# A two-block transformer in float32 on one core: the low part of h's tile 0 gets the same home and the same order of products as the other tiles

## What is computed

```
h = rmsnorm(x, g) * (1 + scale) + shift          # scale, shift, gate from a small product with c
FFN:    y = (silu(h @ w_gate) * (h @ w_up)) @ w_down          # inner width 2816
mixers: y = mixer(h @ w_in) @ w_out
x = x + gate * y
```

## Time and profile before

| | us |
|---|---|
| median of 3 runs | 1773.77 |
| lowest and highest | 1773.6, 1774.51 |
| the profiled execution | 1783.76 |
| its span, first to last instruction | 1782.0 |

### The profile page before, as it was taken

The page is one execution under the profiler, slowest core; times in us unless marked ns, Lnnn a source line. Parts: engine busy times, 40 slices in busy tenths (PEclk is TensorE's granted clock), DMA queues, the critical chain, the costliest instruction groups (busy, mean ns, idle before and its releaser), DMA issues.

```text
span 1782.0 us, 34261 instructions
## 1 busy us (share of the span) xinstructions
PE 1742.4 (98%) x14686; PEld 1699.3 (95%) x14686; DVE 1452.5 (82%) x1750; ACT 956.5 (54%) x1254; POOL 0.2 (0%) x4
## 2 busy tenths in 40 slices
PE   5999999999999999999999999999999999999999
PEld 4999999998999999999999999999999998989999
DVE  7799899988898879897558989765899888567776
ACT  4444566676533454445765333566655556675553
POOL 0000000000000000000000000000000000000000
PEclk9999999999999999999999999999999999999999
DMA  9999734443798859895436988343387545316550
GB/s 395 411 420 332 308 143 166 166 144 141 313 394 328 331 204 389 326 379 183 149 141 227 387 309 352 147 154 124 127 302 282 210 147 187 141 72 218 186 199 34
DMA packets 68149, 426.23 MB, mean 239 GB/s; under 512 B 7488, under 2 KB 10832, under 8 KB 31824
## 3 DMA queue, kind: packets, MB, share of 16 engines
q1 hardware_dynamic: 63936, 416.22, 61.3%
q10 hardware_dynamic: 4112, 8.62, 1.4%
HBM read 423.74 MB, written 3.17 MB: 240 GB/s over the span
## 4 chain that ended last, share of the span: by engine, by line
PE 93%; DVE 3%; ACT 3%; DMA 1%; issue 0%; DVEq 0%; SPq 0%; ACTq 0%
PE bank L1575 25%; PE bank L1576 24%; PE bank L1577 24%; PE bank L1632 2%; PE bank L1634 2%; PE bank L1633 2%; PE bank L1588 1%; PE bank L1688 1%; PE bank L1602 1%; PE bank L1991 1%; DMA mix<-mods 1%; PE bank L1591 1%; ACT w_hi L496 1%; PE bank L1859 1%; ACT work L719 0%; PE bank L1972 0%
## 5 line engine op out<-in xcount | busy, mean ns | idle before, releaser
L1575 PE MATMUL bank<-h_hi,w_hi 128*128 128x256 f32 x2504 | 696.2, 278 | 0.0
L1577 PE MATMUL bank<-h_hi,w_lo 128*128 128x256 f32 x2504 | 695.2, 278 | 0.0
L1576 PE MATMUL bank<-h_lo_rest,w_hi 128*128 128x256 f32 x2504 | 695.2, 278 | 0.0
L915 DVE TENSOR_TENSOR w_lo<-raw,w_hi 128x2048 fp32r<-128x2048 f32 x267 | 609.5, 2284 | 91.4 <-ACT w_hi L496 90.4
L496 ACT ACTIVATE w_hi<-raw 128x2048 fp32r<-128x2048 f32 x276 | 527.9, 1913 | 159.7 <-PE bank L1577 146.1
L1575 PEld LDWEIGHTS bank<-h_hi,w_hi 128*128 128x128 f32 x2504 | 473.0, 189 | 0.0
L1576 PEld LDWEIGHTS bank<-h_lo_rest,w_hi 128*128 128x128 f32 x2504 | 470.2, 188 | 0.0
L1577 PEld LDWEIGHTS bank<-h_hi,w_lo 128*128 128x128 f32 x2504 | 470.1, 188 | 0.0
L1575 PE MATMUL bank<-a_hi,w_hi 128*128 128x256 f32 x1280 | 358.6, 280 | 0.8 <-DVE a_lo L1293 0.8
L1577 PE MATMUL bank<-a_hi,w_lo 128*128 128x256 f32 x1280 | 355.4, 278 | 0.0
L1576 PE MATMUL bank<-a_lo,w_hi 128*128 128x256 f32 x1280 | 355.4, 278 | 0.0
(11 more groups left out here) (304 smaller groups left out, 1986.3 us busy)
## 6 DMA issues: line engine op xcount, KB each, us to landing
raw<-weights SPq DMA_DIRECT2D x276, 1024.0 KB, 5.3
modws<-mods SPq DMA_DIRECT2D x144, 768.0 KB, 6.7
mix<-mods SPq DMA_DIRECT2D x5, 1024.0 KB, 8.8
mix<-mods ACTq DMA_DIRECT2D x8, 512.0 KB, 13.3
biases<-scratch ACTq DMA_DIRECT2D x1, 2048.0 KB, 13.3
mix<-biases ACTq DMA_DIRECT2D x4, 512.0 KB, 3.8
modws<-mods SPq DMA_DIRECT2D x1, 1024.0 KB, 11.6
x<-xin SPq DMA_DIRECT2D x1, 1024.0 KB, 10.9
```

What stands on the lines that cost most here:

```text
L915: eng.tensor_tensor(w_lo[g % NW][:, :], raw[g % NRAW][:, :], w_hi[g % NW][:, :], ALU.subtract).then_inc(sems["wlo"], 1)
L1575: eng.matmul(dst, ah, bh, start=start, stop=False, skip_group_check=skip)
L1576: eng.matmul(dst, ah, bl, start=False, stop=False, skip_group_check=skip)
L1577: return eng.matmul(dst, al, bh, start=False, stop=stop, skip_group_check=skip)
```

## The change

The low parts of all eight tiles lie in one array `h_lo_all`, tile 0 first, so that tile 0 starts at a step of 1024 bytes like the others and tiles 1 to 7 start 1024 bytes later than before. The two gaps become one of 64 floats, and everything behind keeps its address. `gemm` calls `three` for tile 0 too, in both forms. All other lines are the same.

```diff
-        h_lo_rest = sb("h_lo_rest", [P, KT - 1, T], F32R)
-        gap = sb("gap", [P, 16])
-        h_lo_first = sb("h_lo_first", [P, T], F32R)
-        gap2 = sb("gap2", [P, 48])
+        h_lo_all = sb("h_lo_all", [P, KT, T], F32R)
+        gap2 = sb("gap2", [P, 64])

         def h_lo(kk):

-            return h_lo_rest[:, kk - 1, :] if kk else h_lo_first[:, :]
+            return h_lo_all[:, kk, :]
...
-        z_hi, z_lo = h_hi[:, 1:3, :], h_lo_rest[:, 0:2, :]
+        z_hi, z_lo = h_hi[:, 1:3, :], h_lo_all[:, 1:3, :]
...
-                            if tokens and kk == 0:
-                                eng.matmul(d, h_lo(kk)[:, part], hi[:, kk, :], start=True, stop=False)
-                                eng.matmul(d, h_hi[:, kk, part], hi[:, kk, :], start=False, stop=False)
-                                eng.matmul(d, h_hi[:, kk, part], lo[:, kk, :], start=False, stop=False)
-                            elif tokens:
+                            if tokens:
                                 mm = three(d, h_hi[:, kk, part], h_lo(kk)[:, part], hi[:, kk, :], lo[:, kk, :],
                                            kk == 0, kk == KT - 1)
-                            elif kk == 0:
-                                eng.matmul(d, hi[:, kk, part], h_lo(kk), start=True, stop=False)
-                                eng.matmul(d, hi[:, kk, part], h_hi[:, kk, :], start=False, stop=False)
-                                eng.matmul(d, lo[:, kk, part], h_hi[:, kk, :], start=False, stop=False)
                             else:
                                 mm = three(d, hi[:, kk, part], lo[:, kk, part], h_hi[:, kk, :], h_lo(kk),
                                            kk == 0, kk == KT - 1)
```

## The result

| | before | with the change |
|---|---|---|
| median | 1773.97 us (7 runs) | 1792.91 us (7 runs) |
| lowest and highest | 1773.49, 1779.46 | 1780.36, 1794.63 |
| profiled execution, its span | 1783.76, 1782.0 | 1792.91, 1791.1 |
| ratio, 95% interval | | 1.0082 [1.0063, 1.0100] |

The changed kernel is slower, by 0.8% or 14.5 us by the ratio. (The runs of the changed kernel spread over 14 us: four lie between 1792.9 and 1794.7, three between 1780.3 and 1788.7. The ratio is smaller than that of the two medians, 1.0107.) The spread itself is new: six of the seven runs of the kernel before lie between 1773.49 and 1774.7.

A forecast was written before the change was run, and what follows sets the result against it. TensorE, busy 98% of the span, was taken as the bound, through the pace of its matmul starts. Terms -1.1 -1.9 +10.6 -6.4 +4.0 gave +5.2 us on 1773.8: 1779.0 us, range 1764 to 1792.

The forecast's parts named there:

- The mechanism: FFN stages run wholly at a fast or slow pace, 5.3 us apart; tile 0's 64-byte shift switches it.
- the home could not matter: Inference from TensorE's two independent read ports: the change does nothing, 1773.8 us; chance one in fifteen.
- (b): Tile 0's triplet in fast FFN stages: 0.027 us saved each time, 1.1 us for stage 9.
- rival 3: Slower by more: stages 2 and 5 slow, stage 9 slow, or mixers lose re-starts: 1785 to 1792; 0.52 together with forecast.
- (c): Mixers: 94 half-products, some 70 in fast pace, save 0.027 us each: 1.9 us saved.
- (d): Stages 3 and 7 enter slow, nothing turns them fast at L1602, no stall: +5.3 us each, +10.6.
- (e): Stages 2 and 5 enter fast, stall about 0.1 us, then pace open; one of two taken as fast: -6.4 us.
- (f): Stage 0 stays slow to its end without the triplet, if it gets slow at that point again: +4.0 us.
- The sum against the profiled execution: All terms added against the profiled execution's own time of 1783.76 us: +5.2 us.
- I move the difference over unchanged: Profiled execution is 10 us above the runs' median; its +5.2 is applied to 1773.8, giving 1779.0.

The follow-up runs named there:

- e1: Kernel before with tile 0's home kept 64 bytes off, its triplet in plain order (h_hi, h_lo, h_hi): 1776.59 us, ratio 1.0013.
- e2: Changed kernel (low parts in line) with tile 0's triplet issued low part first, as before the change: 1798.85 us, ratio 1.0134.
- e5: Kernel before without the gap: tile 0 keeps its own array and order but lies at a whole 1024-byte step: 1785.21 us, ratio 1.0069.
- e6: Kernel before with the gap doubled, so tile 0 lies 128 bytes off a step instead of 64: 1808.19 us, ratio 1.0193.
- e4: Changed kernel, unedited, profiled a second time: 1799.03 us in one run, five slow stages.
- e8: Changed kernel plus one 64-byte-shifted matmul ahead of each of the first two plain half-products, every stage but the first: 1790.96 us, ratio 1.0084.
- e7: Changed kernel plus one 64-byte-shifted matmul ahead of the first plain half-product of every stage but the first: 1789.35 us, ratio 1.0079.
- e9: Changed kernel plus two matmuls ahead of the low parts of each opening product but stage 0's, to fill TensorE's wait: 1797.53 us, ratio 1.0113.
- e3: Kernel before, unedited, profiled a second time: 1773.36 us in one run, no slow stage.
- e10: Kernel before with plain order in products going to bank 4 (gates), low part first in all others: 1775.24 us, ratio 0.9995.

## Why the prediction was right, and where its sum was not

The sign and the cause were right: slower, by paces that the shifted tile no longer ends. By the ratio the time is 1788.5, inside the range and 9.5 us above the forecast; the median of 1792.91 is 0.9 above its upper end. To lie inside that range says little, for it also held a faster kernel and an unchanged one; the sign was forecast with a chance of 0.52. It was luck that one of stages 2 and 5 came out fast in this very execution, and that what stage 9 cost beyond the forecast and what stage 0 spared offset each other in part.

- **The mechanism** (pace by stage, the address and not the order): shown by e1 and e2, and by e5, where 64 bytes alone are taken away. The page "TensorE: Matmul & The Clock Gate" of the Trainium skill, section "Part 2: What happens when you issue a matmul", says that one read port feeds the streamed operand and the other the weight loads. It says nothing there of what an operand's address does to the pace; that the home could not matter was the prediction's inference, and it fails here by 1.9% (e6) and 0.7% (e5) for a move of 64 bytes. Whether the ports have a part in it no run shows.
- **(b)** The loss of 0.027 us at each tile 0 in fast stages: 0.0266 measured, and 1.1 us a stage. But stage 9, which was to keep its pace, entered slow and stayed so: from its first half-product to the end 180.79 us against 175.31, +5.5 instead of -1.1. This is the part of rival 3 that the forecast left out.
- **(c)** Mixers: -1.9 predicted; the rest of the span, most of it mixers, went from 768.4 to 768.1. The saving is not seen. Stretches that the triplet used to free may have eaten it; that was not separated.
- **(d)** Stages 3 and 7: 169.60 both, +10.6 as worked out, and without a stall, as worked out.
- **(e)** One of stages 2 and 5 fast: stage 5 was, with a stall of 0.12 us where 0.1 was estimated, -6.4. Stage 2 was slow for another reason than the one given: it entered slow. After the stall the pace is indeed open (five slow, four fast).
- **(f)** Stage 0: +4.0 predicted, fast throughout, 170.19 us from the end of the opening product against 170.49. The term was worked out with the condition "if it gets slow at that point again". Here it didn't, though TensorE stood still for 0.95 us at that point (the window has 158.05 us busy of 159); nor in e2, e4, e5 and e8. In e7 it did, and stayed slow: 174.14 against 170.49 is +3.7. In e6 and e9 stage 0 was slow from its start, and 4.7 to 4.9 us longer than in the kernel before, a case that the sum has no term for. The size was right, the condition was not met in this execution.
- **The sum against the profiled execution**: +5.2 predicted, +9.1 measured (span 1782.0 to 1791.1), of which stage 9 is 6.6 more, stage 0 is 4.3 less and the mixers 1.6 more.
- **The step of the sum that failed** is the last one: "I move the difference over unchanged". The profiled execution of before had two slow stages, and that is why it was 10 us longer than the median. A usual run has none (e3), so there the -6.4 of (e) is not to be had: what a fast stage could give is only the 1.1. From e3, the changed kernel's profile costs four slow stages, 4 x 5.3 = 21.2, less 1.1 for the fast stage 5 and some tenths elsewhere: 19.5 measured (1771.6 to 1791.1). The difference between the profile and the runs was itself the effect under study, and it was treated as an offset.

## What to carry over

When the profiled execution is longer than the runs, find what in it is long before taking it as the baseline: durations that come in two sizes for the same work make a run a draw, and an edit must be costed by how it shifts the draws, not by one of them. An edit that looks like tidying of addresses can take away what keeps TensorE out of its slow pace; its cost in the fast case (here 1.1 us a stage) is visible, and its use (5.3 us a stage, at times) isn't. Look at the spread of the runs as well as at the median: 1.3 us for e10, 14 for the changed kernel.

## What the runs showed of the hardware

- The same 1440 matmuls, with no wait and a granted clock of 1.00, take 163.2 or 169.60 us. With the low parts in step the slow pace of stages 2 to 9 holds to the end of the stage, with the same one of every three weight loads at 192 instead of 188 ns. In the FFN stages a pace changed at stalls (as short as 0.03 us in e7) or at reads whose address is off the common step of 1024 bytes (begun and ended in the opening products, begun in stage 5 of e6).
- 64 bytes off in one tile of sixteen: mostly fast. 0: 0.7 to 1.3% slower, with slow and fast stages. 128 bytes off in that tile: 1.9% slower, all six stages slow. 64 bytes off in all eight low tiles: 2.2% slower, five stages slow and stage 0 as long by losses at its triplets. The last two are read from one profile each, and their runs agree within 2 us. No run tells by which rule addresses and loads meet, nor what sets the pace with which a stage is entered; both stay open.
